# Expert rows added in DRAM by an accumulating scatter, h read back from there, a seventh weight slot in h, and small tiles for the router's transposed rows

## The reference

```
h += mixer(rmsnorm(h))
t  = rmsnorm(h)                                   # 512 x 1024
g  = argmax(t @ w_group + b_group)                # one of 4 groups
e1, e2 = top-2 of the 8 experts of that group     # by t @ w_router + b_router
weight_k = softmax(top two logits)_k * softmax(group logits)_g
h += sum over k of weight_k * (silu(t @ w_gate[e_k]) * (t @ w_up[e_k])) @ w_down[e_k]
```

## Time and profile before

| | us |
|---|---|
| median of 3 runs | 1150.05 (1149.61 to 1153.0) |
| the profiled execution | 1149.53 |
| its span, first to last instruction | 1147.7 |
| busy in the span: PE | 1029.5 (90%) |
| busy: DVE, ACT, POOL | 402.8, 255.2, 161.0 |
| mean granted TensorE clock | 0.965 |
| chain of work that ended last: PE, DMA, DVE | 71%, 17%, 5% |

### The profile page before, as it was taken

How to read it: one execution, slowest core, us unless ns; L and a number is a source line. 1 busy time by engine, 2 the same in 40 slices (tenths; PEclk the granted TensorE clock), 3 DMA queues, 4 the chain that set the end, 5 groups by cost and what they waited for, 6 DMA issues and landing times.

```text
span 1147.7 us, 13123 instructions
## 1 busy us (share of the span) xinstructions
PE 1029.5 (90%) x5160; PEld 549.3 (48%) x5160; DVE 402.8 (35%) x1115; ACT 255.2 (22%) x667; POOL 161.0 (14%) x170
## 2 busy tenths in 40 slices
PE   5999999999999999988838998989999999998890
PEld 3344644464455555444414647446455555554440
DVE  3122810362264322222234326458035432322225
ACT  3121710262121111000012226447012111110012
POOL 2000000001003333222111000000102233222210
PEclk9999999999999999999978999999999999998995
DMA  9610202215238999999978210023325999999975
GB/s 330 228 60 25 75 1 110 74 74 190 92 128 339 411 408 410 410 410 411 413 298 289 74 73 1 9 100 116 122 110 194 382 410 410 411 411 410 411 303 230
DMA packets 78814, 268.65 MB, mean 234 GB/s; under 512 B 13664, under 2 KB 17872, under 8 KB 69786
## 3 DMA queue, kind: packets, MB, share of 16 engines
q1 hardware_dynamic: 67056, 248.17, 55.3%
q0 software_dynamic: 11696, 19.62, 4.9%
HBM read 261.41 MB, written 23.10 MB: 248 GB/s over the span
## 4 chain that ended last, share of the span: by engine, by line
PE 71%; DMA 17%; DVE 5%; SPq 4%; ACT 2%; issue 1%; DVEq 0%; POOLq 0%; ACTq 0%
PE bank L735 13%; PE bank L951 12%; DMA W<-in_moe_w_up 10%; PE bank L825 10%; PE bank L747 9%; PE bank L964 7%; PE bank L766 5%; PE bank L777 2%; PE bank L940 2%; PE bank L793 2%; SPq L418 2%; DMA Q<-in_moe_w_up 2%; DMA oT<-in_moe_w_up 2%; PE bank L1071 2%; SPq L413 1%; PE bank L958 1%
## 5 line engine op out<-in xcount | busy, mean ns | idle before, releaser
L951 PE MATMUL bank<-W,K 128*64 128x256 f32 x768 | 186.1, 398 | 27.5 <-DMA W<-in_moe_w_up 25.7
L952 PE MATMUL bank<-W,K 128*64 128x256 f32 x768 | 186.2, 398 | 0.0
L951 PEld LDWEIGHTS bank<-W,K 128*64 128x64 f32 x768 | 105.6, 142 | 87.8 <-DMA W<-in_moe_w_up 29.5
L735 PE MATMUL bank<-hnT,W 128*128 128x512 f32 x336 | 145.1, 593 | 0.8 <-ACT hnT L1145 0.8
L1559 DVE SCALAR_TENSOR_TENSOR PT<-bank,V,PT 64x256 f32<-64x256 f32 x64 | 31.4, 490 | 273.8 <-ACT PT L1209 273.8
L952 PEld LDWEIGHTS bank<-W,K 128*64 128x64 f32 x768 | 105.6, 142 | 0.0
L735 PEld LDWEIGHTS bank<-hnT,W 128*128 128x128 f32 x336 | 63.5, 190 | 80.5 <-issue 79.5
L964 PE MATMUL bank<-D,PT 128*64 128x512 f32 x192 | 92.6, 604 | 0.7 <-ACT PT L1213 0.7
L966 PE MATMUL bank<-D,PT 128*64 128x512 f32 x192 | 92.6, 604 | 0.0
L587 POOL DMA_INDIRECT K<-rows,V x64 | 66.4, 1037 | 147.7 <-DVE V L1479 124.1
L1209 ACT ACTIVATE PT<-bank,V 64x256 f32<-64x256 f32 x64 | 29.9, 468 | 254.4 <-PE bank L952 251.8
(11 more groups left out here) (226 smaller groups left out, 1431.2 us busy)
## 6 DMA issues: line engine op xcount, KB each, us to landing
D<-in_moe_w_down SPq DMA_DIRECT2D x48, 1024.0 KB, 22.1
W<-in_moe_w_gate SPq DMA_DIRECT2D x48, 1024.0 KB
W<-in_moe_w_up SPq DMA_DIRECT2D x48, 1024.0 KB
hnT<-in_moe_w_down SPq DMA_DIRECT2D x16, 1024.0 KB, 21.7
W<-in_e_w_in SPq DMA_DIRECT2D x5, 2048.0 KB
Q<-in_moe_w_gate SPq DMA_DIRECT2D x8, 1024.0 KB
Q<-in_moe_w_up SPq DMA_DIRECT2D x8, 1024.0 KB
oT<-in_moe_w_gate SPq DMA_DIRECT2D x8, 1024.0 KB
```

The lines of the kernel that those rows point to most:

```text
L735: last = nc.tensor.matmul(b[:, :], w[:, k, 128 * fb:128 * fb + 128], hnT[:, k, :], start=(k == 0), stop=(k == KD - 1))
L951: nc.tensor.matmul(bank[2 + e2][0:64, 0:256], xt, w[:, at:at + 256], start=first, stop=end)
L952: last = nc.tensor.matmul(bank[2 + e2][64:128, 0:256], xt, w[:, 2048 + at:2304 + at], start=first, stop=end)
```

## The change

- The scatter becomes an accumulating one: POOL's indirect DMA adds each expert row to the token's row in a DRAM tensor `sums` (2 MB). SP stores h to `sums` right behind each store to `rows`. Two adds may meet in one row, so POOL waits for the landing of each add before it issues the next; all count on one semaphore. The gather's indices serve for the adds too, and the second index column goes.
- h is loaded back from `sums` (four DMAs of 512 KB) instead of the two rows of each token; DVE's eight additions go.
- h's buffer is therefore free during the experts and, with a new tile D4, becomes the seventh slot. The last experts, from 21 on, rotate over four slots.
- The router's transposed rows go to two small tiles `rT` instead of hnT, so T0 and T1 are free earlier: the downs of experts 4, 5 and 6 are loaded during attention. Gate and up of expert 6 are issued once the first gather has landed and h has been stored, squared and transposed.
- ACT and PE do the router's steps in another order, and the area for the descriptors of POOL's DMAs is made smaller (4096 bytes a partition), which makes room for D4.

Index arithmetic of the constants, the further tiles and the places of small tiles within V are left out below.

```diff
@@ buffers
-    y_dram = [nc.dram_tensor(f"expert_rows{l}", (2 * 2 * S, DM // 2), f32, kind="Internal").ap() for l in range(2)]
+    sum_dram = [nc.dram_tensor(f"sums{l}", (2 * S, DM // 2), f32, kind="Internal").ap() for l in range(2)]
-    NSLOT = 6
-    SLOT_W = [("W2", "W3", "W0", "W1", "Q", "oT"), ("W2", "W3", "W1", "W0", "Q", "oT")]
-    SLOT_D = ("D0", "D1", "D3", "D2", "T1", "T0")
+    NSLOT = 7
+    SLOT_W = [("W2", "W3", "W0", "W1", "Q", "oT", "h"), ("W2", "W3", "W1", "W0", "Q", "oT", "h")]
+    SLOT_D = ("D0", "D1", "D3", "D2", "T1", "T0", "D4")
     def slot_of(e):
-        return e % NSLOT if e < 24 else (e - 24) % 4
+        return e % NSLOT if e < 21 else (e - 21) % 4
-        D = [sb(f"D{i}", [128, 2048]) for i in range(4)]
+        D = [sb(f"D{i}", [128, 2048]) for i in range(5)]
+        rT = [PT[:, 768:1280].rearrange("p (k t) -> p k t", k=4), flatV[:, 1536:2048].rearrange("p (k t) -> p k t", k=4)]
-        y_in = [flatQ[:, 0:2048], flatK[:, 0:2048], flatQ[:, 2048:4096], flatK[:, 2048:4096]]
@@ SP, before_routing
                 for c in range(C):
                     sp.wait_ge(s_oga, 8 * lay + 5 + c)
                     sp.dma_start(rows[128 * c:128 * c + 128, :], h[:, c, :]).then_inc(s_hst, 16)
+                    sp.dma_start(sums[128 * c:128 * c + 128, :], h[:, c, :]).then_inc(s_sum, 16)
                 sp.wait_ge(s_og, 8 * lay + 8)
                 load_gate_up(lay, 5)
                 sp.wait_ge(s_g[0], 16 * (8 * lay + 1))
-                sp.wait_ge(s_lg, C * (lay + 1))
-                load_down(lay, 4)
-                load_down(lay, 5)
+                sp.wait_ge(s_hst, 64 * (lay + 1))
+                sp.wait_ge(s_sum, 64 * (lay + 1))
+                sp.wait_ge(s_sqrt, 8 * (lay + 1))
+                sp.wait_ge(s_rtb, 4 * (lay + 1))
+                load_gate_up(lay, 6)
@@ SP, experts
-                for e in range(6, NE):
+                for e in range(NSLOT, NE):
                     sp.wait_ge(s_gu, base + slot_before(e) + 1)
                     load_gate_up(lay, e)
-                    if e > 6:
+                    if e > NSLOT:
                         sp.wait_ge(s_y, base + slot_before(e - 1) + 1)
                         load_down(lay, e - 1)
@@ SP, after the experts
-            def load_expert_rows(lay):
...
+            def load_sums(lay):
+                sp.wait_ge(s_sc, 16 * NE * (lay + 1))
+                sums = sum_dram[lay].rearrange("(s h) d -> s (h d)", h=2)
+                for c in range(C):
+                    sp.dma_start(h[:, c, :], sums[128 * c:128 * c + 128, :]).then_inc(s_yld[c], 16)
@@ SP, layer 0 (before layer 1's experts: load_down(1, e) for e in (0, 1, 6, 2), and 4, 5 after load_gate_up(1, 3))
-            load_down(0, 0)
-            load_down(0, 1)
+            for e in (0, 1, 6):
+                load_down(0, e)
...
             load_gate_up(0, 3)
+            load_down(0, 4)
+            load_down(0, 5)
             before_routing(0, ewout_v)
             experts(0)
-            sp.wait_ge(s_gu, 24)
+            sp.wait_ge(s_gu, 20)
             load_cols("oT", odd_tile[0], owin_v, 0, 512)
-            sp.wait_ge(s_gu, 29)
+            sp.wait_ge(s_gu, 30)
@@ POOL
-            def scatter(lay, src, idx_col, done):
-                pool.indirect_dma_start(out=y_dram[lay],
+            def add_rows(lay, src, idx_col, done):
+                pool.indirect_dma_start(out=sum_dram[lay],
                                         out_offset=bass.IndirectOffsetOnAxis(ap=idx_col, axis=0),
-                                        in_=src, in_offset=None,
-                                        bounds_check=last_result, oob_is_err=False).then_inc(done, 16)
+                                        in_=src, in_offset=None, bounds_check=last_half_row, oob_is_err=False,
+                                        compute_op=ALU.add).then_inc(done, 16)
...
                     if e:
                         pool.wait_ge(s_ye, base + e)
-                        scatter(lay, Y[(e - 1) % 4], sidx[:, e - 1:e], s_sc[(e - 1) % 4])
+                        if e == 1:
+                            pool.wait_ge(s_sum, 64 * (lay + 1))
+                        if base + e > 1:
+                            pool.wait_ge(s_sc, 16 * (base + e - 1))
+                        add_rows(lay, Y[(e - 1) % 4], gidx[:, e - 1:e], s_sc)
@@ PE, mixer_out: order inside the second half, and the logits' operand
-                        last = nc.tensor.matmul(bank[(6, 2)[c % 2]][:, 0:36], hnT[:, k, 128 * c:128 * c + 128],
+                        last = nc.tensor.matmul(bank[(6, 2)[c % 2]][:, 0:36], rT[half][:, k % 4, :],
...
-                        if half:
-                            if c:
-                                second_half(c - 1)
-                            else:
-                                first_half(3)
-                        elif c:
+                        if half and c:
                             first_half(c - 1)
+                            second_half(c - 1)
...
+                        if half and c == 3:
+                            first_half(3)
@@ ACT, roots_for_router
+                nc.scalar.activation(warm[:, 3:4], eps[0:1, 0:1], ACT.Sqrt)
+                for c in range(C - 1):
+                    squares(2 * lay + 1, c)
+                    rows_t_out(c)
+                    root(2 * lay + 1, c)
+                rows_t_out(C - 1)
+                mean_root(2 * lay + 1, C - 1)
@@ DVE
-                for q, idx in enumerate((gidx, sidx)):
-                    ins = nc.vector.tensor_scalar(idx, bank[5][:, NE * q:NE * q + NE],
-                                                  cst[:, C_FIRST + q:C_FIRST + q + 1], None, ALU.add)
-                ins.then_inc(s_idx, 1)
+                nc.vector.tensor_scalar(gidx, bank[5][:, 0:NE], cst[:, C_FIRST:C_FIRST + 1], None, ALU.add)\
+                  .then_inc(s_idx, 1)
...
                     if base + e >= 4:
-                        dve.wait_ge(s_sc[e % 4], 16 * (8 * lay + e // 4))
+                        dve.wait_ge(s_sc, 16 * (base + e - 3))
...
-            def add_expert_rows(lay):
+            def norm_sums(lay):
                 for c in range(C):
-                    dve.wait_ge(s_yld[c], 16 * (lay + 1))
-                    then(nc.vector.tensor_tensor(h[:, c, :], h[:, c, :], y_in[c][:, 0:DM], ALU.add))
-                    if c == 0:
-                        dve.wait_ge(s_yhalf, 16 * (lay + 1))
-                    nc.vector.tensor_tensor(h[:, c, :], h[:, c, :], y_in[c][:, DM:2 * DM], ALU.add).then_inc(s_yadd, 1)
-                    if c:
-                        norm_chunk(2 * lay + 2, c - 1)
-                    if c >= 2 and lay == 0:
-                        norm_out(2, c - 2)
-                norm_chunk(2 * lay + 2, C - 1)
...
+                    norm_chunk(2 * lay + 2, c)
+                    if c and lay == 0:
+                        norm_out(2, c - 1)
@@ building the program
-    nc = bacc.Bacc("TRN2", target_bir_lowering=False, num_devices=1)
+    nc = bacc.Bacc("TRN2", target_bir_lowering=False, num_devices=1, dynamic_dma_scratch_size=4096)
```

More of the change, by code:

```diff
@@ L61, in shape_constants @@
         t[:, C_TOK + 4 * k:C_TOK + 4 * k + 4] = 2 * tok
[L62 to L67, removed]
+        t[:, C_TOK + 8 + 4 * k:C_TOK + 12 + 4 * k] = 2 * tok
+        t[:, C_SLOT + 4 * k:C_SLOT + 4 * k + 4] = 2 * tok - 2 * S
+    t[:, C_FIRST:C_FIRST + 1] = 2 * S + (p >= 64)
     t[:, C_OOB:C_OOB + 1] = OOB + (p >= 64)
@@ L224, in trunk @@
         rbias = flatV[:, 1312:1348]
[L225 to L233, removed]
+        wtab, rtab = flatV[:, 1348:1380], flatV[:, 1380:1412]
+        gidx = flatV[:, 1412:1444].bitcast(i32)
+        router_gain, rows_gain = flatV[:, 1444:1452], flatV[:, 1452:1460].rearrange("p (h k) -> p h k", h=2)
+        slot = flatV[:, 1460:1468].bitcast(i32)
+        orec = flatV[:, 1468:1472].bitcast(i32)
+        oidx = flatV[:, 1472:1473].bitcast(i32)
+        rec = flatV[:, 1476:1508].bitcast(i32)
+        rT = [PT[:, 768:1280].rearrange("p (k t) -> p k t", k=4), flatV[:, 1536:2048].rearrange("p (k t) -> p k t", k=4)]
         zf_w = D[2][:, 0:64].rearrange("p (k n) -> p k n", k=KD)
@@ L362, in trunk @@
         s_ye = sem("down_out")
-        s_sc = [sem(f"rows_scattered{i}") for i in range(4)]
+        s_sc = sem("rows_added")
         ov = [{n: sem(f"further{l}_{n}") for n in
@@ L366, in trunk @@
                 "y", "ye", "down", "scattered", "out", "init", "table")} for l in range(2)]
-        s_yld = [sem(f"expert_rows_loaded{c}") for c in range(C)]
-        s_yadd = sem("expert_rows_added")
+        s_yld = [sem(f"sums_loaded{c}") for c in range(C)]
         s_out = sem("output_stored")
@@ L428, in before_routing @@
                 load_gate_up(lay, 4)
-                rows = h_dram[lay].rearrange("(s h) d -> s (h d)", h=2)
+                rows, sums = [v[lay].rearrange("(s h) d -> s (h d)", h=2) for v in (h_dram, sum_dram)]
                 for c in range(C):
@@ L520, in _ @@
```

(44 more changed lines are left out.)

46 lines of the change are left out of this document (17 added, 29 removed).

## The result

The changed kernel takes 1194.21 us (median of 4 runs, 1192.51 to 1194.49) against 1150.98 us for the kernel before on the same chip (4 runs, 1149.61 to 1153.0). The ratio is 1.0369, with a 95% interval of 1.0354 to 1.0385: it is slower by 43 us, where 1140 us were forecast, and it lies outside the range of 1124 to 1181. The profiled execution took 1192.51 us with a span of 1190.5; the span before was 1147.7. The difference to explain is 42.8 us.

A forecast was written before the change was run, and what follows sets the result against it. Weight loads saturating DMA were taken to bound the expert runs, with 22.7 us of waits a layer. +5.7 + 0.6 - 6.6 - 9.4 - 0.4 = -10.1 from 1149.5 gave 1139.4, forecast 1140 us; range 1124 to 1181.

The forecast's parts named there:

- Step 3: Chain of adds on POOL, each awaiting the last: 7.7 us an add amid weights; last landings +5.7 and +0.6 us.
- the third rival: In POOL's wait before each add: the chain of adds becomes the bound, slower, 8.9 us an add, 1183 us; chance 0.28.
- the two signs that were named against the forecast: In the expert stage: an add of over 8 us amid the weights; a last expert held by anything but its weights.
- Step 2: DMA engines amid the weights: an add's read of its destination costs 5 us a layer, range 0 to 10.2.
- Step 1: Weight loads: three downs move ahead into attention, taking 7.7 us a layer out of the saturated stretch.
- Step 4: End of each MoE, after the last landing: shorter load and no DVE additions gain 6.6 and 9.4 us.
- Step 5: Router, before the first gather: one index column fewer saves 0.2 us a layer; its reordering costs 0.
- The first rival: Scatters to DRAM: the add is as quick as a scatter, 0 cost in DMA time and chain, 1122 us; chance 0.15.

The follow-up runs named there:

- slots_add: Against slots: each scatter accumulates, into rows of its own that are zeroed early, with no wait between adds; 1162.32 us, 1.0086 of the kernel before.
- slots: Changed kernel without the adds: plain scatters to rows of their own, DVE adds, h read back from stored rows; 1135.92 us, 0.9854 of the kernel before.
- after_plain: Changed kernel with its wait, but a plain scatter in place of the add, so the addition is left out; 1133.05 us, 0.9832 of the kernel before.

## Why the prediction was wrong

**Step 3 failed**, in its price of a link: 7.7 us were taken, 8.76 are measured. The mechanism is the one that it describes, and the outcome is the third rival, the chain that becomes the bound. Of the two signs that were named against the forecast one came plainly, a last expert held by something else than its weights, and the other at its edge: loaded adds take 8.0 us in the mean.

- Under load I took 6.6 + 0.8 + 0.3 = 7.7 us; measured are 7.9 in the median from issue to landing and 0.73 to go on, and 8.76 from add to add. The surcharge for the read was 1.3 and more (7.9 to 8.3 against 6.6, also in the kernel without a wait), not 0.8. The nearest row, a larger load amid weights, priced the bytes; it says nothing of a transfer that reads its destination. The 0.3 came from a release by DVE; no row showed how long POOL takes after a DMA it has waited for. The two make 1.06 us a link, 0.4 of it the going on and 0.6 the landing (8.0 in the mean of the loaded links).
- The unloaded link was 5.0 us (5.2 in the second layer) for the 4.6 and 3.1 I took.
- I let 27.4 adds be in when the weights ended, a time (574.3) taken from the weights alone. At 8.76 us the chain delays the slots, the loads stop for 26 us, expert 31's gate and up are issued only at 569.18 and the next stage's loads at 579.11 and 582.76. SiLU of the last expert is at 597.24, not about 577.6, and 26 links are run at the loaded price.
- The link's price is the larger error. With the weights' end kept at 574.3, 210.8/8.76 = 24.1 adds are in, 7.9 are left at 5.0 us, and the last lands at 614: 18.6 us of the first layer's 25. The later end of the loads makes the other 6.5.

From first add to last landing this makes 257.1 us in place of the 232.0 of step 3 (363.53 to 595.5), +25.1; in the second layer 256.3 in place of 224.7, +31.6. Together that is 56.7; the span missed by 52.9 (+42.8 in place of -10.1), since the other steps came out 3.8 us better. (The 1109.5 of the second layer does not follow from the distance to its first scatter, which gives 1110.2, but from that to its last; it is worth 0.4 us of the forecast.) The rival's own number, 1183, was low for the same reason: it had the right link (8.9) but ended the weights at 579.5 whatever the chain did.

**Step 2**: I took 5 us a layer of a range of 0 to 10.2; slots_add shows 11 (SiLU of expert 31 at 585.90, 5.6 us later than before). The bound from below, a hidden read, is excluded; the bound from above, the same bytes as a load, was the right choice, and a little low. The Trainium skill (Collectives: The Full Stack, "The bandwidth ceiling: the fold count and why AG ≠ RS ≠ AR"), which puts a reduce's cost in its second source read, agrees with this case: 11 us stand beside the 10.2 of the bytes. With 10.2 in step 2 and all else kept the forecast would have been about 1145, still wrong, since the chain decides.

**Step 1** held in the main: from first to last scatter slots gains 7.0 us in the first layer and 5.4 in the second, for the 7.7 that left the stretch. Its first scatter comes 1.6 us later (365.10 against 363.53), so the last one comes 5.4 us earlier. It is real, and in the changed kernel the chain ate it.

**Step 4** held. The view is the timeline of the changed kernel behind the last landing (answers to the earlier trace rows):

```profile
619.91 1.77 SPq L479 DMA_DIRECT2D h<-sums  x4
...
628.52 0.72 PEld L717 LDWEIGHTS bank<-cst,Q 128*128 128x128 f32 x4 [0.30 <-issue]
...
1186.14 1.28 DVE L1325 SCALAR_TENSOR_TENSOR Q<-h,rstd,P 128x1024 f32<-128x1024 f32 x1
```

The second chunk's transposes start 8.6 us after the landing (forecast 9.2, before 15.8): a gain of 7.2, where 6.6 were forecast. (The +7.2 for the first chunk is a slip: 4 + 1.7 + 1.3 is 7.0; measured are 6.8.) The last scaling ends at 1187.42, 10.9 us after 1176.48 (forecast 11.7, before 21.1): 10.2, where 9.4 were forecast.

**Step 5**: in front of the first experts 0.7 us where 0.2 were forecast, too little to matter, and not taken apart further.

The first rival, an add as quick as a scatter, was priced at 1122; after_plain is that kernel in effect and takes 1133. The rule of the other page that I weighed, 2.0 us plus bytes at 436 GB/s (the Trainium skill, DMA: Bandwidth & Descriptors, Anatomy of one DMA), fits the unloaded scatter (2.4) and is off by a factor of three for an add amid weights (7.9).

The best kernel of this study that computes the reference's result is slots: 1135.92 us, 1.5% under the kernel before (0.9854 [0.9833, 0.9875]) and some 5% under the changed one (0.9854/1.0369 = 0.950). It takes the extra slot and leaves the adding to DVE.

## What to carry to other kernels

A wait for a DMA's landing in a loop is priced by the landing time under that loop's own traffic plus the step to go on, and is compared with the pace of an unhindered iteration: when they are within ten per cent, as 6.9 and 7.17 us were here, small errors in the link decide the sign. Once a chain is longer than that pace, do not keep the other stream's end fixed: buffers come free late, loads stop, and more of the chain runs at the loaded price. Let accumulation in DRAM have at least two independent targets, or do it on an engine that has time; DVE was busy for 32% of the span.

## What the runs showed of the hardware

- An accumulating indirect scatter occupies POOL for 1.59 us in place of 1.01, lands in 3.7 us alone (plain 2.4) and in 7.9 to 8.3 amid weights (plain 6.6), and has one more packet for each row of 2 KB.
- Its reads do not show in the profile's megabytes (19.62 and 19.64 in q0), but the other stream pays: 409 to 395 GB/s at a full DMA share, and 11 us a layer for 4.2 MB added.
- POOL goes on some 0.73 us after a DMA has landed; after DVE's release 0.27.
- Wait and add cost 18.6 and 26.4 us apart, and 81.8 together.
